# An RWKV mixer whose key projection changes from fp32 matmuls to three fp32r passes for three of its four column chunks

## What is computed

```python
xx = _token_shift(h) - h
xr, xw, xk, xv, xa, xg = [h + xx * mu[i] for i in range(6)]
r = (xr @ w_r).astype(f32)
k = (xk @ w_k).astype(f32)              # 1024 x 1024: the four "k chunks" of 256 columns
...
kk = heads(k * k_k.astype(f32))
kk = kk / jnp.maximum(jnp.sqrt(jnp.sum(kk * kk, axis=-1, keepdims=True)), 1e-12)
```

## Time and profile before

| | |
|---|---|
| median of 3 runs | 1243.45 us (1243.26 to 1245.73) |
| the profiled execution | 1243.26 us, span 1241.5 us |
| TensorE busy | 1224.7 us (99%) |
| VectorE, ScalarE, GpSimd busy | 43%, 49%, 61% |
| the chain that ended last, by engine | TensorE 92%, VectorE 3%, ScalarE 2% |
| granted TensorE clock | 9 of 10 or more in all 40 slices |

### The profile page before, as it was taken

How to read it: one execution, slowest core, us unless ns; L and a number is a source line. 1 busy time by engine, 2 the same in 40 slices (tenths; PEclk the granted TensorE clock), 3 DMA queues, 4 the chain that set the end, 5 groups by cost and what they waited for, 6 DMA issues and landing times.

```text
span 1241.5 us, 23255 instructions
## 1 busy us (share of the span) xinstructions
PE 1224.7 (99%) x9716; PEld 1069.0 (86%) x9716; DVE 528.6 (43%) x825; ACT 607.3 (49%) x793; POOL 763.4 (61%) x192
## 2 busy tenths in 40 slices
PE   8999999999999999999999999999999999999998
PEld 6888887788988888899898888888888998888887
DVE  4232234655342233342533233255968635422333
ACT  7454444445464444584565444432332455644442
POOL 3988880252388888676379888810035425788884
PEclk9999999999999999999999999999999999999999
DMA  7655554244255555544246555533442013555552
GB/s 294 216 187 200 179 193 147 103 172 143 101 198 200 178 198 189 205 173 160 79 153 215 178 199 186 186 128 110 148 168 94 4 37 122 185 203 179 193 198 72
DMA packets 30588, 200.97 MB, mean 162 GB/s; under 512 B 3376, under 2 KB 5296, under 8 KB 6832
## 3 DMA queue, kind: packets, MB, share of 16 engines
q1 hardware_dynamic: 27776, 195.59, 44.8%
q10 hardware_dynamic: 2736, 4.26, 1.0%
HBM read 197.75 MB, written 2.10 MB: 161 GB/s over the span
## 4 chain that ended last, share of the span: by engine, by line
PE 92%; DVE 3%; ACT 2%; issue 1%; POOL 1%; DMA 1%; SPq 0%; POOLq 0%; DVEq 0%
PE psum L346 25%; PE psum L348 13%; PE psum L337 10%; PE psum L339 10%; PE psum L338 10%; PE psum L979 8%; PE psum L992 3%; PE psum L2921 1%; POOL wlo L3267 1%; PE psum L2801 1%; PE psum L2937 1%; PE psum L334 1%; PE psum L2820 1%; PE psum L592 1%; PE psum L335 1%
## 5 line engine op out<-in xcount | busy, mean ns | idle before, releaser
L3267 POOL TENSOR_TENSOR wlo<-raw,whi 128x2048 fp32r<-128x2048 f32 x158 | 727.2, 4608 | 375.2 <-ACT whi L307 326.8
L346 PE MATMUL psum<-f_both,whi 128*128 128x512 f32 x1408 | 492.2, 393 | 1.7 <-DVE wlo L692 1.7
L307 ACT ACTIVATE whi<-raw 128x2048 fp32r<-128x2048 f32 x157 | 300.5, 1915 | 221.6 <-PE psum L348 169.4
L348 PE MATMUL psum<-f_both,wlo 128*128 128x256 f32 x1408 | 393.7, 280 | 0.0
L346 PEld LDWEIGHTS psum<-f_both,whi 128*128 128x128 f32 x1408 | 264.3, 188 | 60.4 <-DVE wlo L692 2.3
L348 PEld LDWEIGHTS psum<-f_both,wlo 128*128 128x128 f32 x1408 | 264.6, 188 | 1.5
L337 PE MATMUL psum<-whi,ahi 128*128 128x512 f32 x352 | 137.4, 390 | 0.3 <-POOL wlo L3267 0.3
L339 PE MATMUL psum<-whi,alo 128*128 128x512 f32 x352 | 137.0, 389 | 0.0
L338 PE MATMUL psum<-wlo,ahi 128*128 128x512 f32 x352 | 136.9, 389 | 0.0
L902 DVE TENSOR_TENSOR psum<-psum,arena 128x512 f32<-128x512 f32 x43 | 30.1, 700 | 241.8 <-ACT arena L618 241.7
L918 DVE TENSOR_TENSOR alo<-arena,ahi 128x512 fp32r<-128x512 f32 x44 | 95.2, 2163 | 31.7 <-ACT ahi L851 31.7
(11 more groups left out here) (408 smaller groups left out, 1414.0 us busy)
## 6 DMA issues: line engine op xcount, KB each, us to landing
raw<-stream SPq DMA_DIRECT2D x182, 1024.0 KB, 4.9
con<-consts SPq DMA_DIRECT2D x1, 1376.0 KB, 14.3
x<-x_in SPq DMA_DIRECT2D x1, 1024.0 KB, 5.1
raw<-stream SPq DMA_DIRECT2D x2, 512.0 KB, 7.3
kept_x<-x ACTq DMA_DIRECT2D x1, 1024.0 KB, 3.9
x<-kept_x ACTq DMA_DIRECT2D x1, 1024.0 KB, 4.8
out<-x SPq DMA_DIRECT2D x4, 256.0 KB, 2.0
arena<-gm_w_s ACTq DMA_DIRECT2D x1, 512.0 KB
```

The costliest lines, as they stand in the source:

```text
L307: nc.scalar.activation(whi[:, slot, :], raw[:, c % RAW, :], ACT.Copy).then_inc(high_made, 1)
L346: nc.tensor.matmul(psum[:, bank, :].rearrange("p (a n) -> p a n", a=2), whi[w], f_both[:, :, k, :], start=k == 0, stop=False, skip_group_c ...
L348: return nc.tensor.matmul(psum[:, bank, 0:TOK], wlo[w], f_hi[:, k, :], start=False, stop=k == KT - 1, skip_group_check=True)
L3267: nc.gpsimd.tensor_tensor(part(wlo[:, slot, :]), part(raw[:, c % RAW, :]), part(whi[:, slot, :]).bitcast(F32), ALU.subtract)\
```

## The change

- Stream order: rw 5, 6, 4, 7 in place of 4, 5, 6, 7. rw 4 is still used first, and stays plain. rw 5, 6 and 7 become split chunks; rw 7 takes the slot that rw 4's place in the stream leaves unused.
- The mixed input xk gets a high and a low part, `key_hi` and `key_lo`, in an area that is free at that time: four ScalarE copies and four VectorE subtractions, 128x512 each. The subtractions count on in `rw_mixed`, so every later value of it is 4 higher (`mixed(v, k)`).
- TensorE runs the three chunks by `split_by_tiles`: row tile by row tile, both column halves, three passes each.
- ScalarE makes the high part of rw 5 at the end of FFN 2, that of rw 6 behind the first `key_hi`, that of rw 7 behind the fourth, all ahead of the copies to `kx`.
- GpSimd makes the low part of rw 5 when its high part is there; that of rw 6 waits also until all four `key_lo` are made (`rw_mixed` at 12); that of rw 7 comes behind it.
- VectorE: the second mixed input no longer comes ahead of `kk`, but in two groups of four tiles, behind `kk` of the first and of the second k chunk.

```diff
-RWKV_ORDER = [("rw", 0, j) for j in (4, 5, 6, 7)] + [("lora", 0, 0), ("lora", 0, 1)] + \
+RWKV_ORDER = [("rw", 0, j) for j in (5, 6, 4, 7)] + [("lora", 0, 0), ("lora", 0, 1)] + \
...
+RWKV_SPLIT = [("rw", 0, j) for j in (5, 6, 7)]
...
-             if name[0] in ("w_in", "rw") and name not in MIX1_SPLIT or name in (("lora", 0, 0), ("lora", 0, 1))}
-    used_after = {("lora", 0, 2): CH[("rw", 0, 11)] + 0.5, **{("w_out", 0, j): CH[("w_in", 0, 1)] + 0.1 * (j + 1) for j in range(3)}}
+             if name[0] in ("w_in", "rw") and name not in MIX1_SPLIT + RWKV_SPLIT or name in (("lora", 0, 0), ("lora", 0, 1))}
+    used_after = {("rw", 0, 4): CH[("rw", 0, 5)] - 0.5, ("lora", 0, 2): CH[("rw", 0, 11)] + 0.5, **{("w_out", 0, j): CH[("w_in", 0, 1)] + 0.1 * (j + 1) for j in range(3)}}
...
+    SLOT[CH[("rw", 0, 7)]] = SLOT[CH[("rw", 0, 4)]]
...
+            key_hi = below.enter_context(nc.sbuf_tensor("key_hi", [P, KT, TOK], F32R))
+            key_lo = below.enter_context(nc.sbuf_tensor("key_lo", [P, KT, TOK], F32R))
...
@@ ffn_scalar, group
-                    highs.upto(c + 5)
+                    highs.upto(c + 4 if (f, g) == (2, GROUPS - 1) else c + 5)
...
@@ rwkv_scalar, behind the eight scaled copies
+            for b in range(4):
+                eng.wait_ge(s("rw_mixed"), 2 * b + 2)
+                nc.scalar.activation(key_hi[:, 2 * b:2 * b + 2, :], variant_x[0][:, 2 * b:2 * b + 2, :], ACT.Copy).then_inc(s("rw_sq"), 1)
+                if b == 0:
+                    highs.upto(CH[RW(6)])
+            highs.upto(CH[RW(7)])
...
@@ rwkv_vector
             nc.vector.tensor_copy(stat[:, 6:7], stat[:, 5:6]).then_inc(S["rms_scale"], 1)
+            for b in range(4):
+                eng.wait_ge(s("rw_sq"), b + 1)
+                k = slice(2 * b, 2 * b + 2)
+                nc.vector.tensor_tensor(key_lo[:, k, :], variant_x[0][:, k, :], key_hi[:, k, :].bitcast(F32), ALU.subtract)\
+                    .then_inc(s("rw_mixed"), 1)
...
-            mix_variant(1)
             for j in range(4):
                 name = RW(4 + j)
                 eng.wait_ge(bank_read[proj_bank(name)], PROJ[name] // 2 + 1)
                 for k in (2 * j, 2 * j + 1):
                     nc.vector.tensor_scalar(kk[:, k, :], kx[:, k, :], V_AT("k_k", k), None, ALU.mult).then_inc(s("rw_kk"), 1)
+                if j < 2:
+                    for k in range(4 * j, 4 * j + 4):
+                        mix_tile(1, k)
                 if j == 2:
                     unit_kk(0)
...
@@ rwkv_tensor
+            def split_by_tiles(slot, bank):
+
+                for k in range(KT):
+                    eng.wait_ge(s("rw_mixed"), 8 + k // 2 + 1)
+                    for j in range(2):
+                        w = (slice(None), slot, slice(k * 256 + j * P, k * 256 + j * P + P))
+                        mm = three_passes(bank2(bank)[:, j, :], whi[w], wlo[w], key_hi[:, k, :], key_lo[:, k, :], True,
+                                          (k, j) == (0, 0), k == KT - 1, skip=True)
+                return mm
+
             for j in range(4):
-                project(eng, RW(4 + j), plain_columns if j else by_tiles, h=variant_x[0])
+                if j:
+                    project(eng, RW(4 + j), split_by_tiles)
+                else:
+                    project(eng, RW(4), by_tiles, h=variant_x[0])
                 if j:
                     square_sums(j - 1)
...
@@ the GpSimd block, low
+                if names[c] == ("rw", 0, 6):
+                    pool.wait_ge(s("rw_mixed"), 12)
```

More of the change, by code:

```diff
@@ L230, in build @@
             f_hi, f_lo = f_both[:, 0, :, :], f_both[:, 1, :, :]
-            below.enter_context(nc.sbuf_tensor("between", [P, H_AT - 2 * KT * TOK], F32))
+            below.enter_context(nc.sbuf_tensor("below_keys", [P, KT * TOK], F32))
+            key_hi = below.enter_context(nc.sbuf_tensor("key_hi", [P, KT, TOK], F32R))
+            key_lo = below.enter_context(nc.sbuf_tensor("key_lo", [P, KT, TOK], F32R))
+            below.enter_context(nc.sbuf_tensor("between", [P, H_AT - 5 * KT * TOK], F32))
             hhi = below.enter_context(nc.sbuf_tensor("hhi", [P, KT, TOK], F32R))
@@ L959, in build @@
         PROJ = {}
-        for name_ in names:
+        for name_ in (names[c_] for c_ in use_order):
             if name_[0] in ("w_in", "hy_w_in", "rw") and name_ != FOX_NARROW:
@@ L1004, in project @@
                 eng.wait_ge(bank_read[6 + q % 2], q // 2)
-            form(c % RAW if c in PLAIN else c % SPLIT, 6 + q % 2, **kw).then_inc(chunk_used, 1)
+            form(c % RAW if c in PLAIN else SLOT[c], 6 + q % 2, **kw).then_inc(chunk_used, 1)
         def quarter(eng, name, form, part, h):
@@ L2313, in at_level, with mixed @@
             return 10 * m + 2 * n + q
+        def mixed(v, k):
+            return 8 * v + k + 1 + (4 if v else 0)
         def variant_used(eng, v):
@@ L2584, in rwkv_vector @@
             eng.wait_ge(s("rw_kx"), 4)
-            eng.wait_ge(s("rw_mixed"), 48)
+            eng.wait_ge(s("rw_mixed"), mixed(5, 7))
             for k in range(8):
@@ L2799, in first @@
                 for k in range(KT):
-                    eng.wait_ge(s("rw_mixed"), 8 * v + k + 1)
+                    eng.wait_ge(s("rw_mixed"), mixed(v, k))
                     mm = nc.tensor.matmul(psum[0:width, bank, half * 256:half * 256 + 256],
@@ L2806, in square_sums @@
             def square_sums(b):
-                eng.wait_ge(s("rw_sq"), b + 1)
+                eng.wait_ge(s("rw_sq"), 4 + b + 1)
                 nc.tensor.matmul(psum[:, b, :], const("same64"), roots[:, 2 * b:2 * b + 2, :], start=True, stop=True)\
@@ L2811, in made @@
             def made(v):
-                return lambda k: eng.wait_ge(s("rw_mixed"), 8 * v + k + 1)
+                return lambda k: eng.wait_ge(s("rw_mixed"), mixed(v, k))
             def by_tiles(slot, bank, h):
@@ L2851, in rwkv_tensor @@
             second(1)
-            eng.wait_ge(s("rw_mixed"), 40)
+            eng.wait_ge(s("rw_mixed"), mixed(4, 7))
             for part in range(2):
```

## The result

The changed kernel takes 1249.18 us (1247.63 to 1249.81), the kernel before, on the same chip, 1243.45 us (1242.19 to 1245.73), five runs each: a ratio of 1.0042 (95% interval 1.0027 to 1.0056), 0.4% slower. The profiled execution took 1249.34 us, its span is 1247.5 us. The forecast was 1247.2 us, within 1241.0 to 1248.8, so the median lies 0.4 us above its upper end.

The account below looks back on a forecast made before the run. TensorE was taken to bound the kernel, busy 1224.7 of 1241.5 us. A stall of +2.2 us and a clock fall of 1.6 us gave +3.8, 1247.2 us, range 1241.0 to 1248.8 (the forecast case alone 1245.9 to 1248.8).

Parts of the forecast that it names:

- Part 1: TensorE's matmuls: a three-pass chunk takes 5.69 us, 1.22 less than fp32; three chunks give at most 3.66 us.
- Parts 2 and 3: ScalarE's high parts and VectorE's four subtractions: rw 7's high part ends at 835.8, subtractions at 835.85, kx copy at 836.4.
- Part 4: GpSimd's low parts: rw 5's is free; those of rw 6 and rw 7 run without a gap from 835.9 to about 845.
- Part 5: VectorE's two kk instructions of rw 4 meet GpSimd's low parts; square sums start at 845.95, rw 7 ends +2.2 us.
- The held end: Upper bound for kk beside GpSimd: held like two-input instructions for the rest of GpSimd's instruction, instead of passing at 0 us.
- The clock: TensorE's clock falls to the 1.2 GHz level after the 5.8 us stall: 1.6 us taken, bounds 0 to twice that.
- the rest shifts as a block: Behind rw 7, everything later moves by the same amount, with the chain on TensorE to the stretch's end.
- the stall: TensorE idle about 5.8 us from 840.14, ahead of the first square sums; +2.2 us at rw 7's end.
- kk free: Rival: both kk instructions pass beside GpSimd at 836.5; -2.8 us, 1240.7; chance 0.14.
- Second kk in between: Rival: the second kk instruction gets in ahead of the second low part; -2.0 us, 1241.4; chance 0.10.
- Clock holds: Rival: same TensorE stall but no fall of the clock; +2.2 us, 1245.6; chance 0.26.
- The change without effect: Rival: TensorE's matmuls in three passes are no faster than fp32; held to be excluded by the rows.

Follow-up runs that it names:

- the second experiment: The changed kernel with kk computed from PSUM and both kk pairs (rw 4, rw 5) ahead of all eight tiles of the second mixed input; 1240.23 us.
- the filled stall: The changed kernel with twelve unused fp32 products behind rw 5, ahead of the first square sums, to keep TensorE busy; 1246.61 us.
- the third: The changed kernel with the low part of rw 7 also waiting for the two kk instructions of rw 4; 1241.72 us.
- the fifth experiment: The changed kernel with ScalarE's copy to kx put ahead of the high part of rw 7; 1241.88 us.

## Why the prediction was right, and where it fell short

The sign and the mechanism were right; one term of the sum was too small, and one loss wasn't in it.

- **Part 1** said 5.69 us for a chunk. Rw 5 runs from 834.51 to about 840.2, and square sums follow each other in 6.49 us in the kernel without a stall, 5.63 for the chunk. Right, and the 3.66 us are to be had in full (3.73 in the second experiment).
- **Parts 2 and 3**: the high part of rw 7 ends at 835.85 (835.8 said), the last subtraction at 835.85 as said, the copy to kx at 836.34 (836.4). Right.
- **Part 4**: GpSimd from 835.99 for 9.10 us (835.9 to 845 said). Right.
- **Part 5**, the step that decided: its bounds were 0 and the rest of GpSimd's instruction. Its "No row has one from SBUF beside GpSimd" is not so: the reduction at 929.37 and the transpose at 944.90 are such rows, and they passed freely. What no row had is one at the rate of L2545, and the rate, which the prediction went by, still fits every row. The held end was true. Held like the earlier trace rows: 8.88 us for both, the square sums at 845.96 (845.95 said), idle 5.65 us (5.8 said). The rule of the Trainium skill that stands in the prediction (GPSIMD Engine Reference, Specifications) agrees with this trace: 8.88 us in place of 0.60. That entry gives no size; here it is that of GpSimd's two instructions, 9.10 us, and comes from the rows.
- **The clock** is the term that was mis-sized, and the larger of the two things that took the time above the range. It fell, as said, but cost 3.0 us by the records and 2.57 by the medians of the changed kernel and the one with the filled stall, where 1.6 was taken. The 1.6 us came from the opening, where ten records ran slowly; here two square sums and 18 of rw 6's matmuls did, for 5.8 us. Its own upper bound, twice 1.6, covers it.
- **Not in the sum**: what follows 936, net 1.0 us at the end, most of it the pause at 954.39 (1.52 us). The prediction had "the rest shifts as a block" behind rw 7. It does up to 935, at +5.05; then VectorE and GpSimd, and the loads and TensorE's 48 more instructions, met differently.

By terms: said 2.2 for the stall and 1.6 for the clock, 3.8; measured 0.2 (ahead of the mixer, from the opening of this execution) + 1.8 + 3.0 + 1.0 = 6.0 in the span, and 5.7 between the medians.

The rivals: **kk free** is out, by 8.88 us. **Second kk in between** describes what the third and the fifth experiment made (-2.08 and -1.90 at 935, where the rival said -2.0), but not the change, where GpSimd's second request stood first. **Clock holds** describes the filled stall: +2.53 at 935 where it said +2.2, and 1246.6 in place of its 1245.6 with the pause, which is in none of the cases. **The change without effect** is out by the second experiment.

## What to carry to other kernels

Before work is put on an idle GpSimd, list what VectorE runs beside it, and ask of each instruction whether it has two SBUF inputs, or one at the faster rate (0.31 us for 128x256 here, against 0.44 out of PSUM): one that came behind GpSimd's start lasted until GpSimd's instruction ended (up to 4.6 us here, and 8.9 for a pair where a second was queued), however small it was. Where it is on the chain, move the meeting, not the work: read from PSUM, run it before GpSimd starts, or let GpSimd wait for it; each of these turned +5.7 us into -1.2 to -1.7 here, and PSUM with the new order of the mixed tiles into -3.1. Price a stall of the busiest engine with the clock behind it: here the stall itself cost under a third of the loss, and the clock half. And look on, past the place of the change: the 48 more matmuls moved the place where TensorE stopped with nothing in the trace to wait for.

## What the runs showed of the hardware that was not expected

- An idle time of 5.65 us was followed by 5.8 us at the 1.2 GHz level (granted clock 0.73 over 846 to 857), at a price of 2.5 to 3.0 us. Idle times of 1.00, 1.16 and 1.41 us in the same stretch left the matmuls behind them at the full clock (square sums of 1.12 or 1.13 us against 2.08), and keeping TensorE busy with unused products avoided the fall altogether. The length alone does not decide: in the opening 1.94 us of idleness ahead of 10.7 were followed by a granted clock of 0.57 over 12 to 16 in the changed kernel's trace, and 2.03 us at the same place by 1.00 in that of the second experiment.
- Of two VectorE instructions queued behind each other, a queued GpSimd instruction gets in between: 8.88 us for the pair with a second low part queued, 4.64 with none. Instructions of 128x512 with one SBUF input at 0.69 and 0.71 us passed beside GpSimd unheld.
- No packet of the instruction queue moved during the burst of two 1 MB loads issued together (947.5 to 953.6), and TensorE stopped ahead of its 6462nd matmul (the 6463rd in one) until 1.33 to 1.46 us after the next packet had landed: for 1.0 to 1.55 us in the seven kernels with three passes that left the loads together, for 0.24 to 0.30 in the two with 48 matmuls fewer, and not at all in the one that parted the loads.
